# Start of the first layer: root per token on columns, swapped b and c from memory, small operations on GpSimd, no filler ahead of the first turn

## The chip, the cores and the metric

The kernel runs on one core of one Trainium2 chip. The metric is the device time of one execution in microseconds. The time before is 2007.02 us, the median of three runs (2006.3 to 2008.06).

## The reference

Two blocks of a language model run one after the other on 512 tokens of width 1024, all in fp32. The first block's first layer is the stage that the change touches:

```
xn = rms_norm(x, g)                      # x * rsqrt(mean(x*x) + 1e-6) * g, per token
u  = xn @ w_in                           # 1024 x 1024
a_bar = exp(lam * dt)                    # complex, 64 groups x 64 states
b_bar = ((a_bar - 1) / lam) * b          # complex
s_t = a_bar * s_(t-1) + b_bar u_t        # per group of 16 channels, 64 states
y_t = real(c s_t) + d * u_t
out = x + glu(gelu(y) @ w_glu)
```

After it come a gated MLP with a short convolution, an attention layer, a second MLP, and a second block (a Mamba-2 layer, a differential attention layer, a last norm). The change leaves all of these as they are.

## The kernel before, in words

Each engine runs its own program, written out by hand, and the programs meet in semaphores. The order of the first layer is one list, `S5_ORDER`, which every engine walks, doing its own share of each entry. x lies with channels on partitions and tokens on the free axis, so one product of `w_in` (128 output channels, 512 tokens) is eight steps of three matmuls: a weight and an activation are each split into a high and a low part (`wh`, `wl`, `xh`, `xl`), and low times low is left out. ScalarE makes `wh` (L394), VectorE makes `wl` (L405), from the buffer `raw` that SyncE's queue fills. Three buffers of `wh` and `wl` exist, so the split of unit n waits for the product of unit n - 3.

Eight products of `w_in`, "dense" 0 to 7, each go to a PSUM bank (`FIRST`). VectorE multiplies a finished bank by the root `rs` ("use" q, L713) and stores it as `ust`. "use" 2 frees the bank of dense 4, and "use" 4 that of dense 5. A matmul may begin before its root is known; only "use" needs it.

The root in the kernel before: in each step of dense 0 TensorE also multiplies the squares of x by a 128x128 matrix of ones (`sum_first_square`, L643, an fp32 matmul that the trace shows as two), which gives the sum of squares on all 128 partitions. VectorE scales it (`variance`, L693), ScalarE takes ln and exp (L675, L677), VectorE corrects it by a Newton step of three instructions on 128x512 (L682, L685, L687). Elsewhere in the kernel a shorter way exists, per token on columns: `sum_tokens` (four matmuls with one column each, L602), `tokens_variance` (L621), `tokens_root`, `tokens_newton` on 128x4, and `spread_tokens` (four matmuls against the identity, L612), from which ScalarE copies `rs`.

VectorE also prepares the state space layer ("prep" 0 to 7, `prep_dve`): powers of a_bar (`pw`), and the factor (a_bar - 1)/lam times the powers (`cb`, in the trace `coefb`). Partitions 0 to 63 hold one half (real) and 64 to 127 another; b and c come from memory with both halves alike, so `flip` exchanges the real and the imaginary part of `cb` (prep 6) and of `pw` (prep 7) in the upper partitions. "inB" q makes the matrix `Bp` (`combine`, L2264, L2270, L2272, from `cb` and b), "inC" q the matrix `CA` (from `pw` and c). TensorE transposes `Bp` ("turnB" q, L2291), applies it to the inputs ("drive", L2355), and makes the near kernel ("near", L2310). Ahead of some turns TensorE runs filler matmuls, whose result nobody reads (`busy_pe`, L2279); their number is in `BUSY_TURN`.

GpSimd issues eight DMAs (L2740) and then, by the order, the loads of `U` (L2347).

Of the kernel before, what the change touches and what calls it, by code (L numbers as in the profile page):

```python
# [8 lines left out]
P = 128  # L9
# [5 lines left out]
G5 = 64  # L15
# [6 lines left out]
ALU = mybir.AluOpType  # L22
# [75 lines left out]
def s5_order():  # L98


    posts = {3: "0a 1a", 4: "2a 3a"}
    out = [("dense", 0), ("use", 0), ("dense", 1), ("use", 1), ("load", 0), ("prep", 4),
           ("dense", 2), ("use", 2),
           ("load", 1), ("prep", 5), ("dense", 3), ("use", 3), ("prep", 6), ("dense", 4), ("inB", 0), ("turnB", 0),
           ("use", 4), ("dense", 5), ("prep", 7), ("drive", 0), ("inC", 0), ("near", 0), ("loadbc", 3), ("inB", 1),
           ("use", 5), ("turnB", 1), ("swap", 0), ("inC", 1), ("dense", 6), ("near", 1)]
    for q in range(8):
        if q < 4:
            out.append(("loadbc", q + 4))
# [473 lines left out]

BY_TOKEN = {2: 0, 5: 3}
LAST_GROUP = 2
TOKENS_ONLY = {4: 1}


def rows_roots(b):
# [45 lines left out]
def sum_first_square(K, pe, k, bank):  # L637

    if k == 0:
        pe.wait_ge("ld1", 16)  # L640
        take(pe, bank, ("nv", 1))
    pe.wait_ge("sq", k + 1)
    mm = pe.e.matmul(K.bank[bank][:, :], K.con("ones"), K.first_sq[k], start=(k == 0), stop=(k == 7))  # L643
    if k == 7:
        mm.then_inc(K.S["ssum"], 1)


def sum_squares(K, pe, b, bank, by_token=None):
# [142 lines left out]
def ffn_dve(K, dve, layer):  # L791
    up, down = f"up{layer}", f"down{layer}"
    cw, cb = f"fcw{layer}", f"fcb{layer}"
    b = 1 + 2 * layer
    split_lo(K, dve, UNIT[(up, "T", 0, 0)] + 1 + LA)
    variance(K, dve, b, 7, 1e-6)
    split_lo(K, dve, UNIT[(up, "T", 0, 0)] + 2 + LA)
    dve.wait_ge("ny", b + 1)
    newton(K, dve, K.ny[:, :], K.nv[:, :], K.ns[:, :], K.rs[:, :]).then_inc(K.S["rs"], 1)
    for half in range(2):  # L800
        for f in range(half * HALF, (half + 1) * HALF):
# [112 lines left out]

def values_out(K, act, name, half):

    act.wait_ge("rt", 1 if name == "w_kv" else 4)
    act.wait_ge("unit", UNIT[(name, "N", D + half * 512, 6)] + 1)
    for t in range(4):
        act.e.activation(K.Vt[name][:, t, half * 512:(half + 1) * 512], K.bank[VALUE_BANKS[name][half] + t][:, :], ACT.Copy,  # L920
                         scale=K.rt[:, t:t + 1]).then_inc(K.S["vt"], 1)
# [1211 lines left out]
GS = [slice(q * W, (q + 1) * W) for q in range(8)]  # L2133
LOW, UP = slice(0, 64), slice(64, 128)
APART = 5
BUSY_TURN = (5, 3, 0, 1, 0, 0, 1, 1)
BUSY_NEAR = (0, 0, 2, 0, 0, 0, 0, 0)
BUSY_READ = (0, 0, 0, 0, 0, 0, 1, 1)

# [11 lines left out]
def first_mul(K, dve, out, x, y, t):  # L2151
# [10 lines left out]
def flip(K, dve, z, n, s0, s1):

    e = dve.e
    keep = K.Bs[UP, 0:5, :].rearrange("p a b -> p (a b)")[:, 0:G5 * n].rearrange("p (g k) -> p g k", k=n)
    own(K, dve, "dve", e.tensor_copy(keep, z[UP, 0, :, :]))
    own(K, dve, "dve", e.tensor_scalar(z[UP, 0, :, :], z[UP, 1, :, :], s0, None, ALU.mult))
    own(K, dve, "dve", e.tensor_scalar(z[UP, 1, :, :], keep, s1, None, ALU.mult))
    own(K, dve, "dve", e.tensor_scalar(z[LOW, 1, :, :], z[LOW, 1, :, :], -1.0, None, ALU.mult))
# [23 lines left out]
def prep_dve(K, dve, i):  # L2193
# [14 lines left out]
    if i == 1:  # L2208
# [13 lines left out]
        own(K, dve, "dve", e.tensor_tensor(pw[:, 1, :, 1], s(3), s(4), ALU.mult))  # L2222
    if 1 <= i <= 3:
        k = 1 << i - 1
        a, z = slice(1, k + 1), slice(k + 1, 2 * k + 1)
        top = [pw[:, c, :, k:k + 1].broadcast_to([P, G5, k]) for c in range(2)]
        first_mul(K, dve, (pw[:, 0, :, z], pw[:, 1, :, z]), (pw[:, 0, :, a], pw[:, 1, :, a]), top,
                  (cb[:, 0, :, 0:k], cb[:, 1, :, 0:k]))
    if i == 4:
        own(K, dve, "dve", e.tensor_scalar(s(8), pw[:, 0, :, 1], -1.0, None, ALU.add))  # L2230
        own(K, dve, "dve", e.tensor_tensor(s(11), s(8), lre, ALU.mult))
        own(K, dve, "dve", e.tensor_tensor(s(0), pw[:, 1, :, 1], lim, ALU.mult))
        own(K, dve, "dve", e.tensor_tensor(s(11), s(11), s(0), ALU.add))
        own(K, dve, "dve", e.tensor_tensor(s(0), pw[:, 1, :, 1], lre, ALU.mult))
        own(K, dve, "dve", e.tensor_tensor(s(2), s(8), lim, ALU.mult))
        own(K, dve, "dve", e.tensor_tensor(s(0), s(0), s(2), ALU.subtract))
        own(K, dve, "dve", e.tensor_tensor(s(11), s(11), s(7), ALU.mult))
        own(K, dve, "dve", e.tensor_tensor(s(0), s(0), s(7), ALU.mult))
    if i == 5:
        t = [K.Bp[:, 4 * j:4 * j + 4, :].rearrange("p a b -> p (a b)").rearrange("p (g k) -> p g k", k=8)  # L2240
             for j in range(2)]
        b8 = [s(j).unsqueeze(2).broadcast_to([P, G5, 8]) for j in (11, 0)]
        first_mul(K, dve, (cb[:, 0], cb[:, 1]), (pw[:, 0, :, 0:8], pw[:, 1, :, 0:8]), b8, t)
    if i == 6:
        dve.wait_ge("kdz", 128)
        flip(K, dve, cb, 8, 1.0, 1.0)
    if i == 7:
        dve.wait_ge("mat", 1)
        e.memset(K.quarter[:, :], math.pi / 2).then_inc(K.S["prep"], 1)
        flip(K, dve, pw, 9, -1.0, -1.0)  # L2250
# [114 lines left out]
def angles_act(K, act, q):  # L2365

    act.wait_ge("ld5", 16)
    act.wait_ge("pd", 4)
    act.wait_ge("ssum", 1)
    act.wait_ge("rot", 4 * q - 2)  # L2370
    for g in range(W):
        ins = act.e.activation(K.rsc[:, g, :], K.five("count")[:, 0:NC], ACT.Copy,
                               scale=K.tau[:, q * W + g:q * W + g + 1])
    ins.then_inc(K.S["pa"], 1)
# [199 lines left out]
        yield  # L2574


def s5_pe(K, pe):
    x = x_of(K, pe, 0)
    for k, step in enumerate(product_steps(K, pe, "a_w_in", (0,), FIRST[:1], x, (("us", 1),))):
        sum_first_square(K, pe, k, 7)  # L2580
    product(K, pe, "a_w_in", 1, FIRST[1], x, ("us", 2))
    glu = gated_steps(K, pe, x_of(K, pe, 1))
    third = product_steps(K, pe, "a_w_glu", (1,), GLU_V[1:2], x_of(K, pe, 1), (("sgv", 2),))
    for what, q in S5_ORDER:
# [34 lines left out]
def s5_act(K, act):  # L2619
# [9 lines left out]
    prep_act(K, act, 2)  # L2629
    prep_act(K, act, 3)  # L2630
    split_hi(K, act, 1 + LA)
    rsqrt_first(K, act, 0)
    for what, q in S5_ORDER:
        if what == "dense":
            split_hi(K, act, done("a_w_in", q) + LA)
        elif what == "prep" and q == 4:
            angles_act(K, act, 0)
        elif what == "splithigh":
            split_hi(K, act, done("a_w_glu", 1))
# [38 lines left out]
def s5_dve(K, dve):  # L2678
# [612 lines left out]
def _pack(inputs):  # L3291
# [5 lines left out]
    def rep(v):  # L3297
# [67 lines left out]
```

## Time and profile before

| | |
|---|---|
| median of three runs | 2007.02 us |
| the profiled execution | 2003.52 us |
| its span (first to last instruction) | 2001.7 us |
| TensorE busy | 98% of the span |
| VectorE busy | 67% |
| ScalarE busy | 45% |
| GpSimd busy | 12% |
| mean granted TensorE clock | 0.998 |

The span begins with the first instruction and ends with the last; 1.8 us of the profiled execution's own time lie around it. Times in the trace are microseconds from the span's start. A busy matmul in the trace overlaps the next one, so distances between starts tell the price, not durations.

### The profile page before, as it was taken

What the parts mean: (1) busy time and instruction counts of PE and PEld (TensorE: products, weight loads), DVE (VectorE), ACT (ScalarE), POOL (GpSimd) and SP (SyncE); (2) the same over time, 40 slices, a digit from 0 to 9 for tenths busy, and PEclk for the clock granted to TensorE, in tenths of its full rate; (3) what the DMA queues carried; (4) which work ended last, traced back from release to release, by engine and by line L of the source; (5) the groups of instructions that cost most, each with busy time, mean ns of one, the idle gap of its engine ahead of it and who ended that gap; (6) DMA issues with size and microseconds to landing.
All of it is one profiled execution on the core that took longest, in us unless ns stands there. A gap on an engine that the chain in (4) does not pass through costs nothing. (4 is left out here: it accounts for less than half of the span.)

```text
span 2001.7 us, 25071 instructions
## 1 busy us (share of the span) xinstructions
PE 1960.5 (98%) x9470; PEld 1562.4 (78%) x9470; DVE 1337.3 (67%) x1922; ACT 896.0 (45%) x1472; POOL 239.4 (12%) x225
## 2 busy tenths in 40 slices
PE   7999999999999999999999999999999999999997
PEld 5787888888888776788888888778888888886665
DVE  7996477536654448846644664778777778437986
ACT  5574243223233337833322233565554545236773
POOL 3040100000001000010000001133333332000002
PEclk9999999999999999999999999999999999999999
DMA  7455323232233220022323323222222223322112
GB/s 224 114 138 153 107 74 106 81 119 95 82 97 106 95 95 22 1 85 84 96 87 112 104 74 102 93 64 69 79 80 80 84 59 108 98 74 74 37 38 74
DMA packets 79624, 178.35 MB, mean 89 GB/s; under 512 B 17680, under 2 KB 31248, under 8 KB 79504
## 3 DMA queue, kind: packets, MB, share of 16 engines
q1 hardware_dynamic: 75792, 169.92, 27.7%
q0 software_dynamic: 3424, 6.23, 1.3%
q8 instruction: 76, 1.25, 0.3%
q10 hardware_dynamic: 288, 0.59, 0.1%
q14 instruction: 44, 0.36, 0.1%
HBM read 169.43 MB, written 7.27 MB: 88 GB/s over the span
## 5 line engine op out<-in xcount | busy, mean ns | idle before, releaser
L405 DVE TENSOR_TENSOR wl<-raw,wh 128x1024 fp32r<-128x1024 f32 (+3 forms) x337 | 383.7, 1139 | 320.6 <-ACT wh L394 319.9
L434 PE MATMUL psum<-xh,wh 128*128 128x512 f32 x1368 | 540.9, 395 | 0.0
L437 PE MATMUL psum<-xh,wl 128*128 128x512 f32 x1368 | 533.5, 390 | 1.3 <-DVE wl L405 1.3
L435 PE MATMUL psum<-xl,wh 128*128 128x512 f32 x1368 | 532.8, 389 | 0.0
L394 ACT ACTIVATE wh<-raw 128x1024 fp32r<-128x1024 f32 (+3 forms) x337 | 316.0, 939 | 299.7 <-PE psum L437 200.0
L434 PEld LDWEIGHTS psum<-xh,wh 128*128 128x128 f32 x1368 | 256.9, 188 | 58.5 <-issue 3.1
L437 PEld LDWEIGHTS psum<-xh,wl 128*128 128x128 f32 x1368 | 256.8, 188 | 56.6 <-DVE wl L405 2.9
L435 PEld LDWEIGHTS psum<-xl,wh 128*128 128x128 f32 x1368 | 257.0, 188 | 55.4 <-issue 2.6
L582 POOL TENSOR_TENSOR rs<-rs,sq 128x512 f32<-128x512 f32 x41 | 54.3, 1324 | 1103.2 <-ACT sq L567 1103.1
L435 PE MATMUL psum<-fl,wh 128*128 128x512 f32 x352 | 137.0, 389 | 0.0
L437 PE MATMUL psum<-fh,wl 128*128 128x512 f32 x352 | 137.0, 389 | 0.0
L434 PE MATMUL psum<-fh,wh 128*128 128x512 f32 x352 | 137.0, 389 | 0.0
L727 DVE TENSOR_TENSOR h<-h,psum 128x512 f32<-128x512 f32 x88 | 59.9, 682 | 67.5 <-PE psum L437 65.1
L475 PE MATMUL psum<-xh,wh 128*128 128x512 f32 x160 | 66.6, 416 | 11.1 <-ACT wh L394 10.8
L435 PEld LDWEIGHTS psum<-fl,wh 128*128 128x128 f32 x352 | 66.1, 188 | 13.7
L434 PEld LDWEIGHTS psum<-fh,wh 128*128 128x128 f32 x352 | 66.1, 188 | 13.7
L437 PEld LDWEIGHTS psum<-fh,wl 128*128 128x128 f32 x352 | 66.1, 188 | 13.7
L545 ACT ACTIVATE xh<-h,par 128x512 fp32r<-128x512 f32 x64 | 44.1, 715 | 64.2 <-DVE h L727 55.6
L779 ACT ACTIVATE ny<-ny 128x512 f32<-128x512 f32 x22 | 13.9, 632 | 110.3 <-DVE ny L816 110.3
L478 PE MATMUL psum<-xh,wl 128*128 128x512 f32 x160 | 62.9, 393 | 0.0
L476 PE MATMUL psum<-xl,wh 128*128 128x512 f32 x160 | 62.8, 393 | 0.0
L779 ACT ACTIVATE nv<-nv 128x512 f32<-128x512 f32 x22 | 13.9, 632 | 103.3 <-DVE nv L816 103.3
(526 smaller groups left out, 3342.2 us busy)
## 6 DMA issues: line engine op xcount, KB each, us to landing
raw<-d_w SPq DMA_DIRECT2D x224, 512.0 KB, 3.5
raw<-d_w SPq DMA_DIRECT2D x32, 384.0 KB, 3.0
raw<-d_w SPq DMA_DIRECT2D x48, 256.0 KB, 2.6
raw<-d_w SPq DMA_DIRECT2D x32, 320.0 KB, 2.9
Mt<-d_kd SPq DMA_DIRECT2D x64, 64.0 KB, 2.4
bc<-d_bc SPq DMA_DIRECT2D x8, 256.0 KB, 3.3
d_ud<-ust SPq DMA_DIRECT2D x8, 256.0 KB, 3.2
U<-d_ud POOLq DMA_DIRECT2D x64, 32.0 KB, 2.7
```

Of the source, the lines that this page charges most:

```text
L394: act.e.activation(K.wh[n % NH][:, 0:COLS[n]], K.raw[n % RAW][:, 0:COLS[n]], ACT.Copy).then_inc(K.S["hi"], 1)
L405: dve.e.tensor_tensor(K.wl[n % NH][:, 0:COLS[n]], K.raw[n % RAW][:, 0:COLS[n]], K.wh[n % NH][:, 0:COLS[n]].bitcast(F32), ALU.subtract).the ...
L434: pe.e.matmul(b[:, :], WH[:, o:o + P], XH, start=(k == k0), stop=False)
L435: pe.e.matmul(b[:, :], WH[:, o:o + P], XL, start=False, stop=False)
L437: mm = pe.e.matmul(b[:, :], WL[:, o:o + P], XH, start=False, stop=(k == k1 - 1))
L475: pe.e.matmul(b[:, :], WH[:, o:o + P], XH, start=(k == 0), stop=False)
L476: pe.e.matmul(b[:, :], WH[:, o:o + P], XL, start=False, stop=False)
L478: mm = pe.e.matmul(b[:, :], WL[:, o:o + P], XH, start=False, stop=(k == 7))
L545: act.e.activation(K.xh[:, k, :], K.h[:, k, :], ACT.Copy, scale=K.par(gain, k)).then_inc(K.S["xh"], 1)
L582: pool.e.tensor_tensor(K.acc[:, :], K.acc[:, :], K.sq[k % 2][:, :], ALU.add).then_inc(K.S["acc"], 1)
L727: dve.e.tensor_tensor(K.h[:, m, :], K.h[:, m, :], K.bank[bank][:, :], ALU.add).then_inc(K.S[signal], 1)
L779: act.e.activation(t[:, :], t[:, :], ACT.Silu).then_inc(K.S["silu"], 1)
```

## The change

- The root of the first norm is made per token on columns. `sum_first_square` runs four one-column matmuls for each of the eight squares; `tokens_variance`, `tokens_root` and `tokens_newton` replace the 128x512 ones; `first_spread` runs within dense 1, behind its step k = 4, and ScalarE copies bank 2 to `rs`.
- b and c lie in memory with the upper partitions holding them in exchanged order, so `flip` is gone. Prep 6 keeps one sign change of 64 partitions, prep 7 two sign changes (one of 128, one of 64 partitions).
- The nine small operations of prep 4 go to GpSimd (`prep_pool`), ahead of its loads of `U`. VectorE waits for them ahead of prep 5 (`pd` 6).
- The order of the Newton step and prep 3 on VectorE is exchanged.
- The five filler matmuls ahead of the first turn are left out.

```diff
-    mm = pe.e.matmul(K.bank[bank][:, :], K.con("ones"), K.first_sq[k], start=(k == 0), stop=(k == 7))
+    for t in range(4):
+        mm = pe.e.matmul(K.bank[bank][:, t:t + 1], K.first_sq[k][:, t * P:(t + 1) * P], K.con("ones")[:, 0:1],
+                         start=(k == 0 and t == 0), stop=(k == 7), skip_group_check=True)
...
-BUSY_TURN = (5, 3, 0, 1, 0, 0, 1, 1)
+BUSY_TURN = (0, 3, 0, 1, 0, 0, 1, 1)
...
-    if i == 4:
-        own(K, dve, "dve", e.tensor_scalar(s(8), pw[:, 0, :, 1], -1.0, None, ALU.add))
...
     if i == 5:
+        dve.wait_ge("pd", 6)
...
     if i == 6:
+        own(K, dve, "dve", e.tensor_scalar(cb[LOW, 1], cb[LOW, 1], -1.0, None, ALU.mult))
         dve.wait_ge("kdz", 128)
-        flip(K, dve, cb, 8, 1.0, 1.0)
     if i == 7:
-        dve.wait_ge("mat", 1)
         e.memset(K.quarter[:, :], math.pi / 2).then_inc(K.S["prep"], 1)
-        flip(K, dve, pw, 9, -1.0, -1.0)
+        e.tensor_scalar(pw[:, 1], pw[:, 1], -1.0, None, ALU.mult)
+        own(K, dve, "dve", e.tensor_scalar(pw[UP, 0], pw[UP, 0], -1.0, None, ALU.mult))
...
+def prep_pool(K, pool):
+    pool.wait_ge("pd", 5)
+    own(K, pool, "pool", e.tensor_scalar(s(8), pw[:, 0, :, 1], -1.0, None, ALU.add))
...
+    e.tensor_tensor(s(0), s(0), s(7), ALU.mult).then_inc(K.S["pd"], 1)
...
+def first_spread(K, pe):
+    spread_tokens(K, pe, 0, 2, ("rs", 1))
...
-    product(K, pe, "a_w_in", 1, FIRST[1], x, ("us", 2))
+    product(K, pe, "a_w_in", 1, FIRST[1], x, ("us", 2), between=(4, first_spread))
...
-    rsqrt_first(K, act, 0)
+    tokens_root(K, act, 0)
...
+            if q == 0:
+                act.wait_ge("ssum", 1)
+                act.e.activation(K.rs[:, :], K.bank[2][:, :], ACT.Copy).then_inc(K.S["rs"], 1)
...
-    variance(K, dve, 0, 7, 1e-6)
+    tokens_variance(K, dve, 0, 7, 1e-6)
     split_lo(K, dve, 1 + LA)
+    tokens_newton(K, dve, 0)
     prep_dve(K, dve, 3)
-    dve.wait_ge("ny", 1)
-    newton(K, dve, K.ny[:, :], K.nv[:, :], K.ns[:, :], K.rs[:, :]).then_inc(K.S["rs"], 1)
...
+    prep_pool(K, pool)
```

## Rows read from the trace of the kernel before

**Rows 1.** The page, part 1: busy time of each engine.
```profile
PE 1960.5 (98%) x9470; PEld 1562.4 (78%) x9470; DVE 1337.3 (67%) x1922; ACT 896.0 (45%) x1472; POOL 239.4 (12%) x225
```

**Rows 2.** Waits of TensorE, 0 to 130 us: total, times, longest.
```profile
PE psum L475 <- ACT wh L394: 10.8, 1, 10.8
PE psum L2291 <- DVE Bp L2272: 2.9, 3, 1.8
```

**Rows 3.** Timeline of TensorE, 0 to 80 us: start, length, instruction, idle before.
```profile
12.52 1.91 PE L643 MATMUL psum<-rs,con 128*128 128x512 f32 x2
...
15.48 1.02 PE L643 MATMUL psum<-sq,con 128*128 128x512 f32 x2
...
17.04 1.02 PE L643 MATMUL psum<-sq,con 128*128 128x512 f32 x2
...
25.25 0.80 PE L434 MATMUL psum<-xh,wh 128*128 128x512 f32 x1
...
36.34 0.39 PE L437 MATMUL psum<-xh,wl 128*128 128x512 f32 x1
...
47.44 4.45 PE L2279 MATMUL psum<-con 128*128 128x512 f32 x10
52.28 1.09 PE L2291 MATMUL psum<-con,Bp 128*128 128x128 f32 x8 [0.38 <-DVE Bp L2272]
...
58.70 1.89 PE L2355 MATMUL psum<-U,BT 128*128 128x64 f32 x16
61.11 1.50 PE L2310 MATMUL psum<-CA,Bp 128*16 128x128 f32 x16 [0.52 <-DVE CA L2272]
...
78.68 1.09 PE L2291 MATMUL psum<-con,Bp 128*128 128x128 f32 x8 [1.77 <-DVE Bp L2272]
```

**Rows 4.** Timeline of VectorE, 25 to 56 us.
```profile
25.93 0.69 DVE L693 TENSOR_SCALAR nv<-psum 128x512 f32<-128x512 f32 x1
...
30.47 0.69 DVE L682 SCALAR_TENSOR_TENSOR xs<-ny 128x512 f32<-128x512 f32 x1
...
32.65 0.69 DVE L713 TENSOR_TENSOR ust<-psum,rs 128x512 f32<-128x512 f32 x1
...
34.99 0.21 DVE L2230 TENSOR_SCALAR s5small<-pw 128x64 f32<-128x64 f32 x1
...
37.41 1.23 DVE L405 TENSOR_TENSOR wl<-raw,wh 128x1024 fp32r<-128x1024 f32 x1
38.55 0.69 DVE L713 TENSOR_TENSOR ust<-psum,rs 128x512 f32<-128x512 f32 x1
...
45.36 0.52 DVE L2166 COPY Bs<-coefb 64x512 f32<-64x512 f32 x1
...
47.47 1.23 DVE L405 TENSOR_TENSOR wl<-raw,wh 128x1024 fp32r<-128x1024 f32 x1
...
51.00 1.22 DVE L2272 TENSOR_TENSOR Bp<-Bp,Bs 128x1024 f32<-128x1024 f32 x1
...
54.01 0.46 DVE L2166 COPY Bs<-pw 64x576 f32<-64x576 f32 x1
...
55.98 0.43 DVE L2412 TENSOR_SCALAR rot<-sq 128x512 f32<-128x512 f32 x1
```

**Rows 5.** Timeline of all engines, 1268 to 1272 us, where a root per token is made.
```profile
1268.68 0.95 PE L602 MATMUL psum<-con,rs 128*128 128x1 f32 x8
...
1269.66 0.16 DVE L621 TENSOR_SCALAR xs<-psum 128x4 f32<-128x4 f32 x1 [7.44 <-PE psum L602]
...
1270.34 0.16 DVE L682 SCALAR_TENSOR_TENSOR xs<-xs 128x4 f32<-128x4 f32 x1 [0.26 <-ACT xs L634]
...
1270.95 1.16 PE L612 MATMUL psum<-con,par 128*128 128x128 f32 x8
...
1271.86 0.48 PE L1370 MATMUL psum<-xh,wh 128*32 128x512 f32 x1
```

**Rows 6.** Groups of GpSimd's instructions by form: busy us, mean ns, idle before.
```profile
L582 POOL TENSOR_TENSOR rs<-rs,sq 128x512 f32<-128x512 f32 x41 | 54.3, 1324 | 1103.2 <-ACT sq L567 1103.1
```

More of the change, by code:

```diff
@@ L101, in s5_order @@
     posts = {3: "0a 1a", 4: "2a 3a"}
-    out = [("dense", 0), ("use", 0), ("dense", 1), ("use", 1), ("load", 0), ("prep", 4),
+    out = [("dense", 0), ("use", 0), ("dense", 1), ("use", 1), ("load", 0), ("angles", 0),
            ("dense", 2), ("use", 2),
@@ L582, in add_squares @@
         pool.e.tensor_tensor(K.acc[:, :], K.acc[:, :], K.sq[k % 2][:, :], ALU.add).then_inc(K.S["acc"], 1)
-BY_TOKEN = {2: 0, 5: 3}
-LAST_GROUP = 2
-TOKENS_ONLY = {4: 1}
+BY_TOKEN = {2: 1, 5: 4}
+LAST_GROUP = 3
+TOKENS_ONLY = {0: 0, 4: 2}
 def rows_roots(b):
@@ L640, in sum_first_square @@
         pe.wait_ge("ld1", 16)
-        take(pe, bank, ("nv", 1))
+        take(pe, bank, ("tv", 1))
     pe.wait_ge("sq", k + 1)
-    mm = pe.e.matmul(K.bank[bank][:, :], K.con("ones"), K.first_sq[k], start=(k == 0), stop=(k == 7))
+    for t in range(4):
+        mm = pe.e.matmul(K.bank[bank][:, t:t + 1], K.first_sq[k][:, t * P:(t + 1) * P], K.con("ones")[:, 0:1],
+                         start=(k == 0 and t == 0), stop=(k == 7), skip_group_check=True)
     if k == 7:
-        mm.then_inc(K.S["ssum"], 1)
+        mm.then_inc(K.S["tsum"], 1)
 def sum_squares(K, pe, b, bank, by_token=None):
@@ L797, in ffn_dve @@
     split_lo(K, dve, UNIT[(up, "T", 0, 0)] + 2 + LA)
-    dve.wait_ge("ny", b + 1)
+    dve.wait_ge("ny", rows_roots(b))
     newton(K, dve, K.ny[:, :], K.nv[:, :], K.ns[:, :], K.rs[:, :]).then_inc(K.S["rs"], 1)
@@ L915, in values_out @@
 def values_out(K, act, name, half):
-    act.wait_ge("rt", 1 if name == "w_kv" else 4)
+    act.wait_ge("rt", 2 if name == "w_kv" else 5)
     act.wait_ge("unit", UNIT[(name, "N", D + half * 512, 6)] + 1)
@@ L2159, in first_mul @@
     own(K, dve, "dve", e.tensor_tensor(out[1], out[1], t[1], ALU.add))
[L2162 to L2169, printed above, removed]
 def prep_act(K, act, i):
@@ L2221, in prep_dve @@
         e.tensor_tensor(pw[:, 0, :, 1], s(3), s(5), ALU.mult)
-        own(K, dve, "dve", e.tensor_tensor(pw[:, 1, :, 1], s(3), s(4), ALU.mult))
+        e.tensor_tensor(pw[:, 1, :, 1], s(3), s(4), ALU.mult).then_inc(K.S["pd"], 1)
+        dve.wait_ge("pd", 5)
     if 1 <= i <= 3:
@@ L2228, in prep_dve @@
                   (cb[:, 0, :, 0:k], cb[:, 1, :, 0:k]))
-    if i == 4:
-        own(K, dve, "dve", e.tensor_scalar(s(8), pw[:, 0, :, 1], -1.0, None, ALU.add))
[L2231 to L2238, printed above, removed]
     if i == 5:
+        dve.wait_ge("pd", 6)
         t = [K.Bp[:, 4 * j:4 * j + 4, :].rearrange("p a b -> p (a b)").rearrange("p (g k) -> p g k", k=8)
@@ L2244, in prep_dve @@
     if i == 6:
+        own(K, dve, "dve", e.tensor_scalar(cb[LOW, 1], cb[LOW, 1], -1.0, None, ALU.mult))
         dve.wait_ge("kdz", 128)
-        flip(K, dve, cb, 8, 1.0, 1.0)
     if i == 7:
-        dve.wait_ge("mat", 1)
         e.memset(K.quarter[:, :], math.pi / 2).then_inc(K.S["prep"], 1)
-        flip(K, dve, pw, 9, -1.0, -1.0)
+        e.tensor_scalar(pw[:, 1], pw[:, 1], -1.0, None, ALU.mult)
+        own(K, dve, "dve", e.tensor_scalar(pw[UP, 0], pw[UP, 0], -1.0, None, ALU.mult))
+def prep_pool(K, pool):
+    e, pw = pool.e, K.pw
+    s = lambda j: K.sm[:, j, :]
+    lre, lim = K.five("lre"), K.five("lim")
+    pool.wait_ge("pd", 5)
+    own(K, pool, "pool", e.tensor_scalar(s(8), pw[:, 0, :, 1], -1.0, None, ALU.add))
+    own(K, pool, "pool", e.tensor_tensor(s(11), s(8), lre, ALU.mult))
+    own(K, pool, "pool", e.tensor_tensor(s(0), pw[:, 1, :, 1], lim, ALU.mult))
+    own(K, pool, "pool", e.tensor_tensor(s(11), s(11), s(0), ALU.add))
+    own(K, pool, "pool", e.tensor_tensor(s(0), pw[:, 1, :, 1], lre, ALU.mult))
+    own(K, pool, "pool", e.tensor_tensor(s(2), s(8), lim, ALU.mult))
+    own(K, pool, "pool", e.tensor_tensor(s(0), s(0), s(2), ALU.subtract))
+    own(K, pool, "pool", e.tensor_tensor(s(11), s(11), s(7), ALU.mult))
+    e.tensor_tensor(s(0), s(0), s(7), ALU.mult).then_inc(K.S["pd"], 1)
 def by_lag(t, n):
@@ L2368, in angles_act @@
     act.wait_ge("pd", 4)
-    act.wait_ge("ssum", 1)
+    act.wait_ge("tsum", 1)
     act.wait_ge("rot", 4 * q - 2)
@@ L2635, in s5_act @@
             split_hi(K, act, done("a_w_in", q) + LA)
-        elif what == "prep" and q == 4:
+            if q == 0:
+                act.wait_ge("ssum", 1)
+                act.e.activation(K.rs[:, :], K.bank[2][:, :], ACT.Copy).then_inc(K.S["rs"], 1)
+        elif what == "angles":
             angles_act(K, act, 0)
@@ L3318, in _pack @@
                                 dtype=np.float32)
-    b = [np.tile(np.transpose(f[n][0], (1, 0, 2)), (2, 1, 1)) for n in ("a_b_re", "a_b_im")]
-    c = [np.tile(np.transpose(f[n][0], (2, 0, 1)), (2, 1, 1)) for n in ("a_c_re", "a_c_im")]
-    bc5 = np.ascontiguousarray(np.stack(b + c, axis=1))
+    b = [np.transpose(f[n][0], (1, 0, 2)) for n in ("a_b_re", "a_b_im")]
+    c = [np.transpose(f[n][0], (2, 0, 1)) for n in ("a_c_re", "a_c_im")]
+    bc5 = np.ascontiguousarray(np.concatenate([np.stack(b + c, axis=1), np.stack(b[::-1] + c[::-1], axis=1)], axis=0))
     xT = f["x"][0].T
```

## The prediction

> **What bounds the kernel now.** I read the page first: TensorE is busy for 98% of the span [rows 1], so the kernel ends when TensorE has got through its list, and a change elsewhere counts only by what TensorE starts earlier or no longer runs. Then TensorE's waits over the first 130 us. After the first 10.8 us, which the change leaves alone, the ones that matter are for `Bp`, 2.9 us in three waits [rows 2]. Then TensorE's timeline: from 25.25 us dense 1 to 4 run without a gap until 47.44 (four products, 22.2 us, 5.44 each and 0.4 of a late start behind an fp32 matmul). Then come 4.45 us of filler and a wait of 0.38, and the first turn starts at 52.28 [rows 3]. So between 47.44 and 52.28 TensorE does nothing that is needed: 4.84 us. What ends that time is VectorE, whose last instruction for `Bp` runs from 51.00 to 52.22, and which has no gap from 25.93 on [rows 4]. The same pair meets again at "near" (`CA` at 61.11, wait 0.52) and at the third turn (78.68, wait 1.77) [rows 3]. The question is how much earlier `Bp`, and then `CA`, are ready, and whether TensorE is there by then.
>
> **VectorE up to "use" 2.** Between the start of the variance (25.93) and that of "use" 2 (38.55) lie 12.62 us without a gap [rows 4]. The change takes away: of the variance some 0.5 (0.6 from start to start for a 128x512, against 0.08 to 0.16 for the 128x4 [rows 4, 5]); of the Newton step 2.18 (30.47 to 32.65) less some 0.55 for three of 0.16 with their waits, so 1.6; prep 4, nine instructions, 34.99 to 37.41, so 2.42. Sum 4.5: VectorE could reach "use" 2 at 34.0, and at 35.5 at the latest if it waits for ScalarE, which now copies `rs` ahead of the splits of units 3 and 4. But "use" 2 needs dense 2, whose last matmul ends at 36.34 + 0.39 = 36.73 now [rows 3]. So from here on VectorE is tied to TensorE, and some 2 us of the 4.5 find nothing to do.
>
> **TensorE up to dense 2.** A step of dense 0 takes 17.04 - 15.48 = 1.56 us, three matmuls of 0.227 and 0.87 for the ones [rows 3]. Four one-column matmuls (eight in the trace) take 0.81 where they occur, which their weight loads set [rows 5]. That is 0.06 less, over the seven later steps 0.4. The first one runs at the slow start: 1.91 for the pair of ones against 1.02 later, that is about 1.7 from start to start [rows 3]; no row shows one-column matmuls there. If they scale they cost 1.6, if they don't 0.8; I take the middle, 0.4 to 0.5 less. The spread in dense 1 is new: 1270.95 to 1271.86 is 0.91, and the next matmul is 0.1 longer [rows 5], so 1.0 more. It must not wait: k = 4 of dense 1 is done at about 25.2 + 3.4 = 28.6, while `rt` is ready at 27.7 (variance at 25.93, split until 27.2, Newton 0.55). Net, dense 2 ends 0.2 us later (bounds: 0.3 earlier, 0.6 later), at 36.93. "Use" 0 needs `rs`: spread done by 29.7, copy by 30.4, while VectorE is through prep 3 at about 30.4 (it ended by 30.47 before, and starts at 27.6 again). Covered, and with it 2 us of slack behind.
>
> **From "use" 2 to the first turn.** "Use" 2 starts at 36.97 instead of 38.55: 1.55 us earlier. Prep 5 and the split stay. Prep 6 was 45.36 to 47.47, 2.11, plus 0.1 of a longer step ahead of it; one operation of 64x512 stays, 0.5. That is 1.6 to 1.7. `Bp` is ready 3.2 us earlier: turn at 52.28 - 3.2 = 49.1. TensorE is there at 47.6 and waits 1.4 without filler. So of the 4.84 the change gets 3.2.
>
> **From the first turn to near.** Prep 7 was 54.01 to 55.98, 1.97 [rows 4]. Two tensor_scalar remain, some 0.45 each, 0.95 in all: `CA` comes 3.2 + 1.0 = 4.2 earlier, at 56.9. TensorE, 3.2 earlier through dense 5 and drive (58.70 + 1.89 = 60.59 now), is there at 57.4: the wait of 0.52 is gone, and near starts 0.45 earlier still [rows 3]. 3.2 + 0.45 = 3.65. VectorE waits for near before it may write `Bp` again, so both now go on 3.65 earlier; the wait of 1.77 at the third turn stays, since VectorE is full up to it. Loads and stores hang on the same semaphores and move along.
>
> **GpSimd.** The nine operations start when their eight DMAs are issued, at about 23.7, and are due at prep 5, at 37.6. No row has a 128x64 on GpSimd; the nearest is 1.32 us for 128x512 [rows 6]. Even at this price nine take 11.9 and end at 35.6; if they cost what VectorE paid, 2.4 (0.27 each). Both ends are hidden, and the loads of `U` behind them started at 36.77. If VectorE's instructions were slowed meanwhile, it would fall into the 2 us before "use" 2. The Trainium skill (GPSIMD Engine Reference, section Specifications) says that GpSimd's SBUF interface is shared with VectorE, with contention when VectorE has two inputs in SBUF, as most of these have. By that rule both get slower for as long as the nine last; no number is needed for it as long as the slack stands.
>
> **Sum.** -1.55 (earlier "use" 2) - 1.65 (prep 6) - 0.45 (near) = -3.65 us. The profiled execution, 2003.5, becomes 1999.9, and its span 1998.0. The median of the runs is 3.5 above the profiled execution; against it, 2007.0 - 3.65 = 2003.4. The bounds of the sum (dense 2 from 0.3 earlier than before to 0.6 later) are 3.25 to 4.15.
>
> **Rivals.**
> 1. *TensorE's clock stays low through dense 0: slower.* The engine starts at half rate (pair of ones 1.91 against 1.02) and is at full rate by about 15.4 us [rows 3]. Now over half of each step is matmuls with one column. If that holds the clock at 1.2 GHz, a step costs three times 0.43 and 0.8 to 1.6, that is 2.1 to 2.9 instead of 1.49, over six steps 3.6 to 8.4 us later, and all of it goes through dense 2 and "use" 2. From 3.65 us on it decides. Time: 2007 to 2012, say 2009.5. For it: no row shows a rise in such a mixture. Against it: drive's 128x64 matmuls keep a distance of 0.12 (16 in 1.89), so few columns for each weight load do not slow the engine there [rows 3]. Chance 0.12. The Trainium skill (TensorE: Matmul & The Clock Gate, section "What's actually happening") has it that the default state is throttled and activity releases it; that speaks for this rival, and the trace agrees as far as the first 4.6 us go.
> 2. *The filler held the clock.* Then the turn and dense 5 run at half rate; for as long as at the start (from 10.8 [rows 2] to about 15.4, 4.6 us) this costs 2.3 us: gain 1.35, time 2005.7. Against it: TensorE waits 1.77 us ahead of the turn at 78.68, and what follows is at full rate (1.09 for eight, as at 52.28) [rows 3]. Chance 0.06.
> 3. *The gain is given back later*, by a transfer of `U`, `Mt` or `ust` that is not relative to what moved, or by VectorE reaching "use" 2 later than 37. Gain 0 to 2, time 2006. Against it: among the waits of TensorE over the first 130 us no DMA is named as what ended one. Chance 0.10.
> 4. The forecast: chance 0.72. Its own range, with runs that differ by 0.9 either way, is 2002.2 to 2004.8.
>
> **How the numbers follow.** 0.2% is 4.0 us, about what a measurement can tell from no change, and the forecast of 3.65 (0.18%) lies just below. Of its 0.72 I give 0.31 to more than 4.0 and 0.41 to less. Rival 1: 0.09 slower, 0.03 same; rival 2: same; rival 3: 0.09 same, 0.01 slower. Faster 0.31, same 0.59, slower 0.10. The range reaches from 2001.9 (a gain of 4.15 and 0.9 of spread) up to rival 3, 2006.8; rival 1 lies outside.
>
> **What would show it.** In the new trace: dense 1 starts at 24.5 to 25.5; dense 2 ends near 36.9; a gap on VectorE of 1.5 to 3 us ahead of "use" 2; the first turn at 49.1, with a wait of 1.2 to 1.6 ahead of it; near at 57.4 with no wait; GpSimd done before 35.6. It is wrong if the steps of dense 0 are 2 us or longer (rival 1), if the spread waits for `rt`, if matmuls behind the first turn are 0.43 apart (rival 2), or if near starts 3.65 earlier and the third turn does not (rival 3).

## The result: 0.33% slower, and the profile after

The changed kernel takes 2012.3 us in the median of 8 runs (2010.9 to 2013.1), the kernel before 2006.2 us in 8 runs (2003.3 to 2008.1). The ratio is 1.0033, with an interval of 1.0024 to 1.0042. The prediction, 2003.4 us, was wrong, and its range too: the time went to rival 1. It comes out just above the 2007 to 2012 us of that rival. The profiled execution took 2013.1 us and its span is 2010.9, 9.2 us longer than the profiled span of before. The medians are only 6.1 apart: the profiled execution of before (2003.5) is one of its fastest and that of the changed kernel its slowest. What the spread of the kernel before goes with is told at the end.

TensorE's timeline of the changed kernel shows all of it. The columns are start, length, instruction, and in brackets the wait before it and what ended it.

```profile
10.85 0.77 PE L475 MATMUL psum<-xh,wh 128*128 128x512 f32 x1 [10.85 <-ACT wh L394]
...
12.61 1.70 PE L644 MATMUL psum<-con,rs 128*128 128x1 f32 x8
...
18.15 0.63 PE L478 MATMUL psum<-xh,wl 128*128 128x512 f32 x1
18.58 1.70 PE L644 MATMUL psum<-con,sq 128*128 128x1 f32 x8
...
33.51 1.70 PE L644 MATMUL psum<-con,H 128*128 128x1 f32 x8
35.08 0.77 PE L434 MATMUL psum<-xh,wh 128*128 128x512 f32 x1
...
36.50 0.63 PE L434 MATMUL psum<-xh,wh 128*128 128x512 f32 x1
...
37.78 0.63 PE L434 MATMUL psum<-xh,wh 128*128 128x512 f32 x1
...
41.39 1.05 PE L612 MATMUL psum<-con,par 128*128 128x128 f32 x8
...
42.51 0.39 PE L435 MATMUL psum<-xl,wh 128*128 128x512 f32 x1
42.74 0.40 PE L437 MATMUL psum<-xh,wl 128*128 128x512 f32 x1
...
62.19 1.06 PE L2291 MATMUL psum<-con,Bp 128*128 128x128 f32 x8 [1.34 <-DVE Bp L2272]
...
70.39 1.50 PE L2310 MATMUL psum<-CA,Bp 128*16 128x128 f32 x16
...
87.96 1.09 PE L2291 MATMUL psum<-con,Bp 128*128 128x128 f32 x8 [1.77 <-DVE Bp L2272]
```

The matmuls of 512 columns lie 0.43 us apart from the first step of dense 0 to step k = 4 of dense 1 (18.15 to 18.58, and 36.50 to 37.78 for three), against 0.23 from 42.51 on: 1.2 GHz against 2.4. The engine did not wait in all that time, and before the first of them it had stood still for 10.85 us. The granted clock in the views does not show this stretch: the trace's record of it begins with full clock at 41.1 us (at 15.4 in the kernel before), and what lies ahead of the record is printed as 1.00. Here is such a stretch of the changed kernel (the columns are the stretch, its length, busy time, granted clock, the DMA engines' mean busy share and what they moved in GB/s):

```profile
20.00:30.00 10.00, 10.00 (x37) 1.00 0.57 88
```

So at the start the distances tell the rate. That 0.43 us means half clock can be seen where both are recorded (experiment 8). A step of dense 0 takes 2.99 us (33.51 - 12.61, over seven), against 1.56 in the kernel before, where full rate was there in the second step [rows 3]. Dense 1 starts at 35.08 instead of 25.25.

From there the three marks tell where the time stays. Dense 2 ends at 49.97, 13.2 us later than the 36.73 of before. The first turn is 9.9 later (62.19 against 52.28), near 9.3 (70.39 against 61.11), the third turn 9.3 (87.96 against 78.68) [rows 3]. So 13.2 us were lost ahead of the end of dense 2, and 3.9 to 4.0 won back behind it, which is what the forecast had promised. The whole span is 9.2 longer, so on balance nothing is lost or won behind the third turn.

VectorE's timeline of the changed kernel, with the gaps that the late TensorE leaves, and the parts that the change made cheaper:

```profile
35.32 0.16 DVE L621 TENSOR_SCALAR xs<-psum 128x4 f32<-128x4 f32 x1 [9.04 <-PE psum L644]
...
50.08 0.69 DVE L715 TENSOR_TENSOR ust<-psum,rs 128x512 f32<-128x512 f32 x1 [1.93 <-PE psum L437]
...
56.77 0.47 DVE L2229 TENSOR_SCALAR coefb<-coefb 64x512 f32<-64x512 f32 x1
57.28 1.23 DVE L405 TENSOR_TENSOR wl<-raw,wh 128x1024 fp32r<-128x1024 f32 x1
```

"Use" 2 starts 0.1 us behind the last matmul of dense 2, where it was 1.8 us behind it before. Prep 6 takes 0.51 us instead of 2.11 [rows 4].

GpSimd's timeline, first and last of the nine small operations:

```profile
23.90 0.58 POOL L2242 TENSOR_SCALAR s5small<-pw 128x64 f32<-128x64 f32 x1
...
27.39 0.32 POOL L2250 TENSOR_TENSOR s5small<-s5small 128x64 f32<-128x64 f32 x1
```

They end at 27.7, 3.8 us in all, far ahead of prep 5.

### The profile page after: what moved, and what is told of

It reads as the page before. It is cut to its first block and busy times, and to the rows that moved or that the text cites. A ratio compares the mean times of both kernels' runs of the same rounds, so it can differ in the third digit from the quotient of the medians.

```text
span 2010.9 us, 25158 instructions
## 1 busy us (share of the span) xinstructions
PE 1969.3 (98%) x9516; PEld 1576.0 (78%) x9516; DVE 1331.2 (66%) x1908; ACT 895.6 (45%) x1473; POOL 242.9 (12%) x234
## 3 DMA queue, kind: packets, MB, share of 16 engines
q1 hardware_dynamic: 75792, 169.92, 27.7%
## 5 line engine op out<-in xcount | busy, mean ns | idle before, releaser
L437 PEld LDWEIGHTS psum<-xh,wl 128*128 128x128 f32 x1368 | 257.4, 188 | 57.2 <-DVE wl L405 3.0
L475 PE MATMUL psum<-xh,wh 128*128 128x512 f32 x160 | 65.8, 412 | 11.2 <-ACT wh L394 10.8
L781 ACT ACTIVATE ny<-ny 128x512 f32<-128x512 f32 x22 | 13.9, 632 | 109.6 <-DVE ny L818 109.6
L781 ACT ACTIVATE nv<-nv 128x512 f32<-128x512 f32 x22 | 13.9, 632 | 104.0 <-DVE nv L818 104.0
```

The source lines that it names most:

```text
L437: mm = pe.e.matmul(b[:, :], WL[:, o:o + P], XH, start=False, stop=(k == k1 - 1))
L475: pe.e.matmul(b[:, :], WH[:, o:o + P], XH, start=(k == 0), stop=False)
L781: act.e.activation(t[:, :], t[:, :], ACT.Silu).then_inc(K.S["silu"], 1)
```

## The experiments

Two theories stood at the start; they have the letters that the expectations use. Theory C: the one-column matmuls in each step of dense 0 keep TensorE at half rate, so dense 0 and 1 run slowly (rival 1). Theory D: something else of the change delays the start (the spread, ScalarE's copy of `rs`, the exchanged order on VectorE, the wait for GpSimd, the missing filler), and the low rate is only a part. The runs came in three groups (1 to 4, 5 to 8, 9 to 12), each on one chip with the kernel before; its median was 2005.7, 2005.6 and 2005.3 us.

### 1. The old root in the changed kernel

The variance, the Newton step and its old place behind prep 3 come back with the sums.

```diff
-    for t in range(4):
-        mm = pe.e.matmul(K.bank[bank][:, t:t + 1], K.first_sq[k][:, t * P:(t + 1) * P], K.con("ones")[:, 0:1],
-                         start=(k == 0 and t == 0), stop=(k == 7), skip_group_check=True)
+    mm = pe.e.matmul(K.bank[bank][:, :], K.con("ones"), K.first_sq[k], start=(k == 0), stop=(k == 7))
...
-            if q == 0:
-                act.wait_ge("ssum", 1)
-                act.e.activation(K.rs[:, :], K.bank[2][:, :], ACT.Copy).then_inc(K.S["rs"], 1)
```

> The changed kernel with the root of the kernel before put back (sums against 128x128 ones, Newton on 128x512); swapped b and c, GpSimd, the sign changes and the missing filler stay. Theory C (the one-column sums hold TensorE's clock at half rate through dense 0): dense 1 starts at 25.3 again as before, the first turn at about 50.2 (use 2 at 36.8 instead of 38.55, prep 6 1.65 shorter, so 3.4 minus some 1.3 for the longer variance and Newton), near 2.5 to 3.9 us earlier than before, end 2.5 to 3.9 us below before (ratio 0.998 to 0.999). Theory D (some other part costs, the wait for GpSimd, the missing filler or the exchanged order): the kernel stays 2 us or more above before.

2002.8 us in the median of 11 runs (1998.0 to 2004.2), ratio 0.9982 (0.9973 to 0.9991). Half rate ends within dense 0 again, at 15.8 us, and dense 1 starts at 25.47. TensorE's timeline of this kernel:

```profile
49.11 1.06 PE L2289 MATMUL psum<-con,Bp 128*128 128x128 f32 x8 [1.26 <-DVE Bp L2270]
...
57.32 1.50 PE L2308 MATMUL psum<-CA,Bp 128*16 128x128 f32 x16
...
74.88 1.09 PE L2289 MATMUL psum<-con,Bp 128*128 128x128 f32 x8 [1.78 <-DVE Bp L2270]
...
165.19 0.41 PE L2474 MATMUL psum<-U,Mt 128*128 128x64 f32 x2 [1.55 <-DMA Mt<-d_kd]
165.43 0.39 PE L2479 MATMUL psum<-H,CA 128*128 128x64 f32 x2
...
166.19 0.64 PE L2474 MATMUL psum<-U,Mt 128*128 128x64 f32 x2
166.61 0.63 PE L2479 MATMUL psum<-H,CA 128*128 128x64 f32 x2
```

Turn at 49.11 with a wait of 1.26, near at 57.32 without one, third turn 3.80 earlier than before: the changed kernel's other parts do what was forecast. The expectation had the turn at 50.2, with 1.3 us set aside for the longer variance and Newton step. They cost nothing, for "use" 2 still has to wait for dense 2; VectorE's timeline of this kernel:

```profile
37.07 0.69 DVE L713 TENSOR_TENSOR ust<-psum,rs 128x512 f32<-128x512 f32 x1 [0.35 <-PE psum L437]
```

So the whole gain that was forecast comes from the other parts of the change, and the root per token adds nothing to it. But here the profiled span is 2001.6, no better than the 2001.7 of before. The lower lines of TensorE's timeline show where it went: behind a wait of 1.55 us for a transfer of `Mt`, pairs of 64 columns go from 0.22 to 0.43 apart, and the windows show it as a granted clock under 1:

```profile
160.00:170.00 10.00, 8.45 (x43) 0.80 0.71 198
170.00:180.00 10.00, 10.00 (x36) 0.69 0.47 128
```

That costs about 4 us in this execution, since 3.8 were won by the third turn and 0.1 is left in the span. Runs of this kernel fall in two heaps: four between 1998.0 and 1999.7 at a mean granted clock of 0.997 or 0.998, seven between 2002.3 and 2004.2 at 0.995 or 0.996. So the gain is there and is in some runs given back far from the change. Theory C holds so far, and a fall of the clock at a second place comes beside it.

### 2. The token root alone in the kernel before

The reverse edit of 1 in the kernel before, and nothing else of the change.

> The kernel before with only the root made per token on columns (one-column sums, spread in dense 1, copy by ScalarE, Newton ahead of prep 3); filler, flips and prep 4 on VectorE stay. Theory C: dense 0 runs in steps of 2.99 us as in the changed kernel, dense 1 starts at 35, dense 2 ends at 50.05, near comes 9.3 + 3.5 = 12 to 14 us later than before, time 9 to 13 us above before, more than the whole change. Theory D: no more than 2 us above before.

2013.8 us in 5 runs (2012.9 to 2014.4), ratio 1.0040 (1.0027 to 1.0053). The steps take 2.99 us again, the first turn starts at 63.51, the third at 89.26, 10.6 later than before. The whole loss comes with the root alone. It is less than expected: near comes 10.6 later and not 12 to 14, and the medians are 8.1 apart and not 9 to 13. The rate rises at 38.0 us here instead of 41.1, so dense 2 ends 11.8 us later than before and not 13.3, and TensorE's waits of 0.38 and 0.52 in the kernel before [rows 3] vanish behind the late start. The third turn is itself at half rate here:

```profile
89.26 1.97 PE L2293 MATMUL psum<-con,Bp 128*128 128x128 f32 x8 [1.78 <-DVE Bp L2274]
```

### 3. Work for TensorE while it waits at the start

The changed kernel, with seven matmuls of 512 columns on a tile of ones, whose result nobody reads, in the 10.8 us in which TensorE has nothing to do. VectorE fills the tile first.

```diff
+    pe.wait_ge("prep", 1)
+    for _ in range(7):
+        pe.e.matmul(K.bank[6][:, :], K.ny[:, 0:P], K.ny[:, :], start=True, stop=True)
...
+    own(K, dve, "dve", dve.e.memset(K.ny[:, :], 1.0))
```

> The changed kernel with seven fp32 matmuls of 512 columns on a tile of ones at the very start, in the 10.8 us in which TensorE has nothing to do, so that dense 0 begins at full clock. Theory C in its form C1 (few columns prevent the rise, but do not bring a high clock down within 12 us): dense 0 in steps of 1.49, dense 1 at 22.8, dense 2 ended by 34.7, the turn bound by VectorE, near 4.5 to 6 us earlier than before, end 4 to 6 us below before. C2 (the mixture also brings a high clock down): the clock falls back within dense 0, steps of 2.99 from there, end 0 to 7 us above before. Theory D: no change against the changed kernel, 6 us above before.

1998.4 us in 12 runs, eleven of them between 1997.8 and 1999.5, ratio 0.9969 (0.9960 to 0.9979): by the medians 13.9 us under the changed kernel and 7.3 under the one before. TensorE's timeline:

```profile
2.78 7.87 PE L2584 MATMUL psum<-ny 128*128 128x512 f32 x14 [2.78 <-DVE Bs L2696]
10.71 0.47 PE L475 MATMUL psum<-xh,wh 128*128 128x512 f32 x1
...
13.79 0.95 PE L644 MATMUL psum<-con,sq 128*128 128x1 f32 x8
...
23.37 0.95 PE L644 MATMUL psum<-con,H 128*128 128x1 f32 x8
...
28.18 1.16 PE L612 MATMUL psum<-con,par 128*128 128x128 f32 x8 [0.30 <-DVE par L689]
...
49.00 1.06 PE L2291 MATMUL psum<-con,Bp 128*128 128x128 f32 x8 [1.27 <-DVE Bp L2272]
...
57.21 1.50 PE L2310 MATMUL psum<-CA,Bp 128*16 128x128 f32 x16
...
74.78 1.09 PE L2291 MATMUL psum<-con,Bp 128*128 128x128 f32 x8 [1.80 <-DVE Bp L2272]
```

The very same steps take 1.60 us ((23.37 - 13.79) / 6) once the engine comes to them at full rate, and it keeps that rate through them. The third turn is 13.18 us earlier than in the changed kernel, and dense 2 ends 13.1 earlier (36.85), which is what was lost. Theory D has nothing left to explain. Against the kernel before, near and the third turn are 3.9 earlier, less than the 4.5 to 6 that the expectation had. The profiled spans are 5.2 apart; the other 1.3 come between the third turn and 200 us, and no experiment looks into them. The rest of the 7.3 is mostly that the median run of before is slower than its profiled one.

### 4. More work in each step

The changed kernel, with one more matmul of 512 columns (two in the trace) behind the one-column ones of each step but the last.

```diff
     if k == 7:
         mm.then_inc(K.S["tsum"], 1)
+    else:
+        pe.e.matmul(K.bank[6][:, :], K.con("ones"), K.first_sq[k], start=True, stop=True)
```

> The changed kernel with work added: behind the four one-column sums of each step but the last, one fp32 matmul of 512 columns against the ones (result unused), 0.87 us at full clock, 1.7 at half. Theory C: the clock rises within dense 0, as in the kernel before, by about 16 us; steps of 2.36 us; dense 1 starts at 28 to 32 instead of 35.1, so more work gives an earlier end than the changed kernel by 3 to 8 us, 2 to 3 us either side of before. Theory D, or a clock that is held down by any one-column matmul: steps of 4.7 us, 15 to 20 us above the changed kernel.

2007.4 us in 11 runs (2006.6 to 2011.8), ratio 1.0012 (1.0003 to 1.0020): slower than before, but less than the changed kernel (1.0033), though it does more. TensorE's timeline:

```profile
12.52 1.70 PE L644 MATMUL psum<-con,rs 128*128 128x1 f32 x8
14.08 2.06 PE L649 MATMUL psum<-rs,con 128*128 128x512 f32 x2
...
17.21 1.70 PE L644 MATMUL psum<-con,sq 128*128 128x1 f32 x8
...
21.79 0.95 PE L644 MATMUL psum<-con,sq 128*128 128x1 f32 x8
```

Two steps of 4.7 and 4.6 us at half rate, then 2.45 us each. The rate rises at about 21.5 us, not at 16 as expected, and dense 1 starts at 34.84, hardly earlier than the 35.08 of the changed kernel: the time is won in dense 1, which runs at full rate from its start. Among the profiles that begin dense 0 from a standstill, the rate rises at 14.9 to 16.2 with the old sums in its steps (the kernel before, 1, 7, 10), at 21.5 here, and at 38.0 and 41.1 with the one-column sums alone beside the product (2, the changed kernel), only when dense 1 is under way.

### 5. The early work in the kernel before

The edit of 3 in the kernel before.

> The kernel before with the seven matmuls at the start (while TensorE has nothing to do) and nothing else of the change. Theory C (the clock at the start, and what it loses, is the story of the change): dense 0 in steps of 1.55 from the first one, dense 1 at about 23.5 instead of 25.25; but the first turn is bound by VectorE, which is without a gap from 25.9, so the turn stays at 52.3 and the end within 1 us of the fastest runs of before, 2003 to 2005, with less spread than before's 2002.8 to 2009.8. Rival (warming the start is worth the 7 us by itself, and the rest of the change nothing): 1998 to 1999 as the changed kernel with warm start.

2006.1 us in 11 runs (2002.5 to 2009.1), ratio 0.9999 (0.9990 to 1.0008); the smaller spread that was expected did not come. Dense 0 does run faster, but the first turn only comes at 51.99 behind a wait of 1.62 us for `Bp`, and the third at 78.41: VectorE sets the time there. So the gain of experiment 3 over the kernel before isn't the early work's own; it needs the shorter VectorE work of the change.

### 6. The early work with the old root

Experiments 1 and 3 together.

> The changed kernel with the old root and with the seven matmuls at the start. If the token root has worth of its own once the clock is no issue: near at 57.2 here too or later by at most 1 (VectorE waits for dense 2 in both), so the token root is worth 0 to 1 us, time 1998 to 1999. If VectorE's longer variance and Newton (2.1 us) bind after all: near 1 to 2 us later, 1999 to 2000.5.

2003.8 us in 12 runs (1999.3 to 2004.8), ratio 0.9987 (0.9979 to 0.9996), at least 3.3 us above what was expected. TensorE's timeline:

```profile
48.62 1.17 PE L2289 MATMUL psum<-con,Bp 128*128 128x128 f32 x8 [2.52 <-DVE Bp L2270]
...
50.02 0.63 PE L435 MATMUL psum<-xl,wh 128*128 128x512 f32 x1
50.45 0.63 PE L437 MATMUL psum<-xh,wl 128*128 128x512 f32 x1
```

TensorE comes to the first turn earlier than in 1 and so waits 2.52 us instead of 1.26, and now the rate falls (0.43 from 50.02 to 50.45): this is the mechanism of rival 2, which the changed kernel itself escapes. The price was 1.1 us at near (58.40 against 57.32), and the fall at 169 to 175 us was there too.

### 7. Two more fillers ahead of the last reading

`BUSY_READ` gives the number of filler matmuls ahead of the eight readings at the end of the layer, where 1 shows its fall; the last one gets three instead of one. First with the old root:

```diff
-BUSY_READ = (0, 0, 0, 0, 0, 0, 1, 1)
+BUSY_READ = (0, 0, 0, 0, 0, 0, 1, 3)
```

> The changed kernel with the old root, and three filler matmuls instead of one ahead of the last reading of the state (they fit in a wait of 1.55 us for a DMA). Without them its profile shows TensorE at half clock from 165.9 to 176.3 us, and runs from 1998.0 to 2004.2 with a median of 2002.8. Theory C extended (this fall takes the 4 to 5 us by which the runs differ): median 1998 to 1999.5. Rival (the runs differ by something else, such as transfers): median 2002 to 2004 as without them.

1999.9 us in 6 runs (1998.7 to 2001.4), ratio 0.9971 (0.9960 to 0.9982), and no mean granted clock under 0.997. The windows of this kernel:

```profile
160.00:170.00 10.00, 9.94 (x54) 1.00 0.71 194
170.00:180.00 10.00, 10.00 (x46) 1.00 0.63 189
```

The upper heap of 1 is gone. So 1 gave back its gain at the last reading.

### 8. The one-column matmuls in one block

The changed kernel, with the 32 one-column matmuls (64 in the trace) behind dense 0 instead of in its steps. This lets the rate rise first.

```diff
-    for k, step in enumerate(product_steps(K, pe, "a_w_in", (0,), FIRST[:1], x, (("us", 1),))):
+    for step in product_steps(K, pe, "a_w_in", (0,), FIRST[:1], x, (("us", 1),)):
+        pass
+    for k in range(8):
         sum_first_square(K, pe, k, 7)
```

> The changed kernel with all 32 one-column sums in one block behind dense 0 instead of four in each step. Theory C: dense 0, now of 512-column matmuls alone, warms up by about 15.5 and ends at 19.5 to 20; the block takes 32 x 0.2 = 6.5 us at full clock, or, if the clock falls within it, up to 13; dense 1 starts at 26 to 28 (up to 33 if it falls); end 0 to 3 us below before (or 2 to 5 above, if it falls). If any one-column matmul were the cause whatever its place: as the changed kernel, 6 us above before.

2007.4 us in 11 runs (2005.6 to 2009.3), ratio 1.0010 (1.0001 to 1.0018). Full rate is reached in dense 0, at 14.94, and lost again in the block. Windows of this kernel over the block, which begins at 19.56:

```profile
21.00:21.50 0.50, 0.50 (x7) 1.00 0.98 229
21.50:22.00 0.50, 0.50 (x5) 0.56 1.00 93
...
23.00:31.00 8.00, 8.00 (x39) 0.50 0.36 33
31.00:35.00 4.00, 4.00 (x11) 0.50 0.01 2
```

The engine's matmuls follow one another without a gap, and still the granted clock goes to a half. The last stretch holds the 512-column matmuls of dense 1, 0.43 us apart: that distance is half clock. So the one-column matmuls in a block let a full rate fall; mixed with three of 512 columns, as in 3, they don't.

### 9 and 10. The fillers of 7, in 3 and in the kernel before

> The changed kernel with the seven matmuls at the start and three filler matmuls instead of one ahead of the last reading. Theory C: as the changed kernel with warm start (1998.4) or up to 0.5 below, all runs within 2 us of each other since neither the start nor the last reading can fall to half clock; 1998 to 1999.5, ratio to before 0.996 to 0.997. Rival (the fillers only cost): 1.5 to 2 us above the warm start alone.

1998.9 us in 6 runs (1998.2 to 1999.6), ratio 0.9969 (0.9957 to 0.9980). Its median is 0.5 us above that of 3, less than the intervals tell apart. All six runs are at 0.998. In 3 one run of twelve took 2007.9 us at 0.993; six runs without such a one don't show that it can't happen here.

> The kernel before with three filler matmuls instead of one ahead of the last reading, nothing of the change. If a fall of the clock there is also what separates the runs of before (2002.6 to 2009.8): median 2002.5 to 2004.5, spread half. Rival (before's spread comes from its start or from elsewhere): median 2005 to 2007, the two fillers cost up to 1.7.

2004.0 us in 11 runs (2002.8 to 2005.0), ratio 0.9993 (0.9984 to 1.0002). The median moves by less than the interval, but the runs lie within 2.2 us, where the 25 of the kernel before beside them lie within 6.4.

### 11. The old root, the early work, and fillers at both places

Experiment 6 with `BUSY_TURN` beginning with 3 and the `BUSY_READ` of 7.

> The changed kernel with the old root, warm start, three fillers ahead of the last reading, and three fillers (of the former five) ahead of the first turn. Without the latter its profile shows a wait of 2.52 us there and half clock from 48.6 to 52.7, near at 58.40 instead of 56.8. Theory (the missing filler costs as soon as TensorE comes early): no half clock behind the first turn, near at 56.9 to 57.3, third turn at 74.4 to 74.9, time 1997.5 to 1999.5 against 2003.8. Rival (it was the wait for VectorE alone): near at 58.4 again, time as without them less the 4 us of the last reading, 1999.5 to 2000.5.

1999.8 us in 8 runs (1998.9 to 2000.7), ratio 0.9973 (0.9962 to 0.9983). The turn starts at 48.83 behind a wait of 0.22, without half rate, and the third turn at 74.60. The median lies 0.3 above the expected range. Of the 3.9 us between the medians of 6 and this, 1.4 lie ahead of the third turn (75.96 against 74.60); the rest fits the fall at 169 to 175 us, which this profile doesn't have. Beside 9 (third turn at 74.84, median 0.9 lower) no worth of the token root at full rate can be told; the two kernels also differ in the three fillers ahead of the turn.

### 12. The squares added on GpSimd

The changed kernel with `BUSY_READ` as in 7, where GpSimd adds the eight squares (seven additions of 128x512), so that TensorE needs only four one-column matmuls, in dense 1, and spreads the root in dense 2.

```diff
+    for k in range(1, 8):
+        pool.wait_ge("sq", k + 1)
+        own(K, pool, "pool", pool.e.tensor_tensor(K.acc[:, :], K.acc[:, :], K.first_sq[k], ALU.add))
...
+    product(K, pe, "a_w_in", 1, FIRST[1], x, ("us", 2), between=(1, first_sum))
```

> The changed kernel where GpSimd adds the eight squares (seven additions of 128x512, 1.3 us each) and TensorE sums them by four one-column matmuls in dense 1 instead of 32 in dense 0; the spread is in dense 2; three fillers ahead of the last reading; no warm start. Theory C: with 512-column matmuls alone the clock is up by 15.5, dense 0 ends at 19.6 (bound by its inputs, 18.7), dense 1 to 4 run 3 to 5 us earlier than before; VectorE then binds, turn at 48 to 49 after a wait of 3 to 5 us, in which the clock may fall for 4 us (2 lost). Time 1996.5 to 2000. If the sums were not what held the clock: dense 0 still at half rate, above 2005.

2007.5 us in 11 runs (2006.2 to 2009.8), ratio 1.0010 (1.0001 to 1.0019), where 1996.5 to 2000 was expected. VectorE's timeline shows why:

```profile
12.79 5.17 DVE L553 SCALAR_TENSOR_TENSOR xl<-h,par,xh 128x512 fp32r<-128x512 f32 x3
17.88 2.31 DVE L405 TENSOR_TENSOR wl<-raw,wh 128x1024 fp32r<-128x1024 f32 x1
20.11 4.09 DVE L553 SCALAR_TENSOR_TENSOR xl<-h,par,xh 128x512 fp32r<-128x512 f32 x3
```

and TensorE's:

```profile
22.00 0.77 PE L475 MATMUL psum<-xh,wh 128*128 128x512 f32 x1 [2.96 <-DVE xl L553]
...
55.74 1.94 PE L2291 MATMUL psum<-con,Bp 128*128 128x128 f32 x8 [3.99 <-DVE Bp L2272]
```

While GpSimd adds (10.1 to 23.0 us, 1.6 to 1.8 us for one and once 2.1, against a mean of 1.32 in [rows 6]), an `xl` of VectorE takes 1.4 to 1.7 us instead of 0.7, and a split 2.3 instead of 1.2. `xl` is late, TensorE waits 2.96 us for it and falls back to half rate. The Trainium skill (GPSIMD Engine Reference, section Specifications) has the two engines share their SBUF interface, with contention when VectorE has two inputs there; these rows agree, with a factor of about two. The turn without filler then waits 3.99 us and is at half rate itself.

## Why the prediction was wrong

**The step that failed** is the price of the sums in dense 0: "over the seven later steps 0.4 [less]. The first one runs at the slow start ... I take the middle, 0.4 to 0.5 less." It took the clock's rise at 15.4 us from the kernel before as given, and so asked about one step at the slow start. The runs show that the rise depends on what the engine is fed with: with four one-column matmuls in each step it came at 38 to 41 us (the changed kernel and 2; with 1, 3 and 4 for the cause), and a step cost 2.99 us instead of the 1.49 of the forecast. Its own sign of being wrong, steps of 2 us or longer, came true. Eight of the one-column records cost 1.57 us at half rate (33.51 to 35.08), the upper end that the prediction named, and 0.81 at full rate.

**Rival 1** named this mechanism, gave it 0.12 and priced it at 2.1 to 2.9 us a step over six steps; measured are 2.99 over eight. It also ended at dense 1, where four more steps and a part of the fifth ran at half rate. The loss is 9.8 us up to dense 1 and 3.4 in dense 1 (some 0.9 of it the spread), 13.2 in all. The reason given against it was drive's 128x64 matmuls, which keep their distance of 0.12 at full rate. That row tells what few columns do to an engine at full rate for 2 us between products; it says nothing on whether the rate rises under one column. The Trainium skill (TensorE: Matmul & The Clock Gate, section "What's actually happening") has throttling as the default, which activity lifts. The trace agrees in the first part, with half rate from 10.85 us on; in the second it differs, for 30 us of matmuls without a gap did not lift it. Rival 1 should have had more weight than 0.12, since nothing in the rows spoke for a rise in such a mixture.

**The rest of the sum** was right. Relative to the end of dense 2, "use" 2 came 1.7 us earlier (forecast 1.8), prep 6 gave 1.60 (forecast 1.6 to 1.7), near gave 0.63 (9.91 - 9.28; forecast 0.45), together 3.9, as forecast (its 3.65 counts dense 2 as 0.2 later). With the clock right the third turn is 3.80 to 3.90 earlier than before (1, 3). The marks hold there too: turn 49.0 to 49.1 with a wait of 1.27, near at 57.2 to 57.3 without one. Part of that is luck: in 3 dense 2 ends at 36.85 beside the forecast's 36.93, but the early work has taken the slow start away, and the spread, which was not to wait, waits 0.30 us and costs 1.45 instead of 1.0. One number of the prediction does not follow from its own: gains of 3.25 to 4.15 with 0.9 us either way give 2001.9 to 2004.7 for the forecast's own range, not 2002.2 to 2004.8. At full rate a step costs 1.60, 0.04 more than before and not 0.06 less, since the first matmul behind the eight starts 0.1 late.

**GpSimd's nine operations** took 3.8 us, between the bounds of 2.4 and 11.9, and were hidden. **Rival 2** did not happen in the changed kernel (the matmuls behind the turn at 62.19 are 0.23 apart), but does when the wait grows to 2.5 us (6) or 4.0 (12). **Rival 3**, a gain given back later, happens with the old root in most runs (1), by a wait for `Mt` and a lower clock behind it, about 4 us. The reason given against it looked at TensorE's waits up to 130 us only; this one is at 165.

**The best version** is the change with the early work (3), with or without the fillers of 9: 1998.4 to 1998.9 us, ratio 0.9969 to the kernel before.

## What to carry to other kernels

Where TensorE comes from a long wait, don't price a new mixture of matmuls at full rate: read from the trace what lifted the clock there, and if the change takes exactly those wide matmuls away, price the stretch at half rate or put wide matmuls into the idle time ahead of it. When a change frees VectorE, its gain is read behind the last mark that TensorE sets, and a filler that can go while the wait is 1.3 us is needed again when TensorE comes earlier and waits 2.5 (6, 11).

## What the runs showed of the hardware

- An engine without any idle time can stay at 1.2 GHz: some 30 us in the changed kernel, of which 24.2 went to steps of eight one-column records (1.57 us) and three of 512 columns (1.42 us) and the last 6 to 512-column matmuls alone. The same steps kept 2.4 GHz when they were entered at it (3). A block of one-column records alone lost it about 2 us behind its start (8). Each one-column matmul also loads 128x128 weights of its own; whether the few columns or these loads keep the rate low, no run tells apart.
- The mean granted clock sorts the runs of the kernel before. Of the 84 in the three groups, the 30 with 0.998 have a median of 2003.8 us, the 15 with 0.997 2004.8, the 24 with 0.996 2006.2, the 15 with 0.995 2008.0. The slow start is not in this mean, which reads 0.997 to 0.998 in the changed kernel too. So much of the spread goes with time at half rate later in the kernel, and two fillers ahead of the last reading take away about two thirds (10). In which of its stages the fall lies in each run, the single profile of before can't show.
- Waits of 1.26 to 1.62 us ahead of the first turn never led to half rate in the profiles (the changed kernel, 1, 3, 4, 5, 7, 8, 9). For the transfer of `Mt`, waits of 1.55 and 1.68 did (1, 6) and one of 1.78 did not (5). One of 1.8 us ahead of the third turn did in three executions (2, 8, 12) and did not in the others. One of 2.52 and one of 3.99 did (6, 12). What else decides below 2 us stays open.
